# A modulation stage turned around: weight tiles as the stationary operand, condition columns streamed

## The reference

```
silu of the condition c and of the context's condition c_ctx   (two vectors of 1024)
for each of 2 layers:  m = silu(cond) @ mod_w[layer] + mod_b[layer]
    mod_w[layer]: 1024 x 6144 float32;  m is cut into six vectors of 1024:
    shift, scale and gate for the mixer, shift, scale and gate for the FFN
h = h * (1 + scale) + shift ;  x = x + gate * y
```

## Time and profile before

| | us |
|---|---|
| median of 3 runs | 5251.93 (5250.98 to 5257.39) |
| span of the profiled execution | 5251.9 |
| modulation stage in it, first matmul to next stage | 39.15 to 216.94 |
| TensorE busy over the span | 4450.2 (85%) |
| VectorE, ScalarE, GpSimd busy | 2259.8, 1628.1, 630.8 |
| matmul records of the stage (L735) | 384, 170.0 busy |
| transposes of the stage (L721) | 96, 9.5 busy |

### The profile page before, as it was taken

One profiled execution on the slowest core, in us unless ns is written; L12 is line 12 of the kernel. 1 busy time (PEld: TensorE's weight loads), 2 busy tenths in 40 slices (PEclk: granted clock), 3 DMA queues, 4 the chain that ended last, 5 costly groups with the idle time before them and its releaser, 6 DMA issues. The chain is left out here.

```text
span 5251.9 us, 53549 instructions
## 1 busy us (share of the span) xinstructions
PE 4450.2 (85%) x21497; PEld 3364.3 (64%) x21497; DVE 2259.8 (43%) x2925; ACT 1628.1 (31%) x2392; POOL 630.8 (12%) x523
## 2 busy tenths in 40 slices
PE   7797967799997887879989699976996969995997
PEld 2285545688875554657777388545785648843876
DVE  0213665311453222263362545455364455355356
ACT  0211452211342111152252233332363233233244
POOL 0000021000000011000000256100000235401000
PEclk9898977899998988989999889888998978886998
DMA  7510001111111111123222000011222100001321
GB/s 257 185 57 23 1 5 33 48 64 64 55 50 43 48 50 42 34 80 96 86 82 85 8 1 1 5 48 57 94 90 64 37 9 1 5 1 49 103 88 64
DMA packets 258876, 290.91 MB, mean 55 GB/s; under 512 B 6891, under 2 KB 230658, under 8 KB 258690
## 3 DMA queue, kind: packets, MB, share of 16 engines
q1 hardware_dynamic: 258689, 288.36, 17.0%
HBM read 286.24 MB, written 2.10 MB: 55 GB/s over the span
## 5 line engine op out<-in xcount | busy, mean ns | idle before, releaser
L421 PE MATMUL banks<-h_halves,w_halves 128*128 128x512 f32 (+1 forms) x4400 | 1627.1, 370 | 92.4 <-DVE w_halves L255 52.7
L422 PE MATMUL banks<-h_halves,w_halves 128*128 128x512 f32 (+1 forms) x4400 | 1626.4, 370 | 0.0
L423 PE MATMUL banks<-h_halves,w_halves 128*128 128x512 f32 (+1 forms) x4400 | 1617.8, 368 | 0.0
L421 PEld LDWEIGHTS banks<-h_halves,w_halves 128*128 128x128 f32 x4400 | 838.0, 190 | 255.1 <-issue 64.9
L423 PEld LDWEIGHTS banks<-h_halves,w_halves 128*128 128x128 f32 x4400 | 835.5, 190 | 141.2
L422 PEld LDWEIGHTS banks<-h_halves,w_halves 128*128 128x128 f32 x4400 | 837.7, 190 | 135.8
L255 DVE TENSOR_TENSOR w_halves<-work,w_halves 128x2048 fp32r<-128x2048 f32 (+1 forms) x215 | 492.1, 2291 | 735.9 <-ACT w_halves L250 735.9
L250 ACT ACTIVATE w_halves<-work 128x2048 fp32r<-128x2048 f32 (+1 forms) x215 | 407.4, 1896 | 292.8 <-PE banks L423 245.6
L250 ACT ACTIVATE h_halves<-kept 128x512 fp32r<-128x512 f32 (+1 forms) x520 | 336.1, 667 | 344.6 <-PE banks L423 266.9
L255 DVE TENSOR_TENSOR h_halves<-kept,h_halves 128x512 fp32r<-128x512 f32 (+1 forms) x520 | 364.9, 737 | 161.9 <-ACT h_halves L250 161.3
L526 ACT ACTIVATE kept<-banks 128x512 f32<-128x512 f32 (+1 forms) x158 | 85.7, 594 | 797.8 <-PE banks L423 797.8
(11 more groups left out here) (297 smaller groups left out, 4627.1 us busy)
## 6 DMA issues: line engine op xcount, KB each, us to landing
work<-in_w_ff SPq DMA_DIRECT2D x64, 1024.0 KB, 5.4
work<-in_mod_w SPq DMA_DIRECT2D x24, 2048.0 KB, 8.0
work<-in_ffn_w_in SPq DMA_DIRECT2D x44, 1024.0 KB, 5.1
work<-in_odd_w_in SPq DMA_DIRECT2D x24, 1024.0 KB, 5.6
work<-in_w_in SPq DMA_DIRECT2D x24, 1024.0 KB, 5.2
work<-in_ffn_w_out SPq DMA_DIRECT2D x16, 1024.0 KB, 5.1
work<-in_even_w_in SPq DMA_DIRECT2D x13, 1024.0 KB, 5.4
work<-in_odd_w_out SPq DMA_DIRECT2D x8, 1024.0 KB, 5.1
```

Source lines behind the costliest of these rows:

```text
L421: nc.tensor.matmul(o, low[:, k - a, fc], rh[:, tc], start=(k == 0), stop=False)
L422: nc.tensor.matmul(o, high[:, k - a, fc], rl[:, tc], start=False, stop=False)
L423: mm = nc.tensor.matmul(o, high[:, k - a, fc], rh[:, tc], start=False, stop=(k == K - 1))
```

## The change

The roles of the two operands are exchanged. For each tile there are 4 blocks of 128 weight columns; for each block, 8 matmuls (one for each k) whose stationary operand is the 128 x 128 block of weights and whose streamed operand is the pair of condition columns. A sum lands as 128 x 2 columns, which is the layout wanted. The 4 blocks fill 8 columns of bank j % 2 (`summed`). ScalarE's row copies, TensorE's transposes and the two semaphores for them are gone. VectorE adds the bias from the sums directly. TensorE now waits for the bias add of tile g - 2 in place of the row copy of g - 2 and the add of g - 4. The loads, the ring of three slots and the order of the tiles stay.

```diff
-    row = lambda b: core.sb(U0 + b * cols, cols, 2)
-    (in0, in1, in2, rows_summed, rows_copied, rows_turned, bias_added) = core.sems(7)
+    (in0, in1, in2, columns_summed, bias_added) = core.sems(5)
...
-    turned = lambda j: core.ps[:, 2 + j % 2, 0:8]
+    summed = lambda j: core.ps[:, j % 2, 0:8]
...
-                        sp.wait_ge(rows_summed, g - slots + 1)
+                        sp.wait_ge(columns_summed, g - slots + 1)
...
-            def turn(g, j):
-
-                for q in range(4):
-                    mm = nc.tensor.transpose(turned(j)[:, 2 * q:2 * q + 2], row(j % 2)[:, q * P:(q + 1) * P],
-                                             core.sb(IDENT0, 2, 2))
-                mm.then_inc(rows_turned, 1)
-
...
                     if later or j >= 2:
-                        pe.wait_ge(rows_copied, g - 1)
-                    if later or j >= 4:
-                        pe.wait_ge(bias_added, g - 3)
-                    for k in range(KD):
-                        mm = nc.tensor.matmul(core.ps[0:2, j % 2, 0:cols], core.sb(COND0 + 2 * k, 2),
-                                              slot(j % slots)[:, k], start=(k == 0), stop=(k == KD - 1))
-                    mm.then_inc(rows_summed, 1)
-                    if later or j >= 2:
-                        turn(g - 2, (j - 2) % body)
+                        pe.wait_ge(bias_added, g - 1)
+                    for q in range(4):
+                        for k in range(KD):
+                            mm = nc.tensor.matmul(summed(j)[:, 2 * q:2 * q + 2], slot(j % slots)[:, k, q * P:(q + 1) * P],
+                                                  core.sb(COND0 + 2 * k, 2), start=(k == 0), stop=(k == KD - 1))
+                    mm.then_inc(columns_summed, 1)
...
-        @block.scalar
-        def _(act):
-            def body_of(layer, i, later):
-                for j in range(body):
-                    g = (layer * R + i) * body + j
-                    act.wait_ge(rows_summed, g + 1)
-                    if later or j >= 2:
-                        act.wait_ge(rows_turned, g - 1)
-                    nc.scalar.activation(row(j % 2), core.ps[0:2, j % 2, 0:cols], ACT.Copy).then_inc(rows_copied, 1)
-            loop(act, body_of)
...
-                    dve.wait_ge(rows_turned, g + 1)
+                    dve.wait_ge(columns_summed, g + 1)
...
-                                            turned(j).rearrange("p (q n) -> p q n", n=2), bias,
+                                            summed(j).rearrange("p (q n) -> p q n", n=2), bias,
```

More of the change, by code:

```diff
@@ L730, in body_of @@
                     if later or j >= 2:
-                        pe.wait_ge(rows_copied, g - 1)
-                    if later or j >= 4:
-                        pe.wait_ge(bias_added, g - 3)
-                    for k in range(KD):
-                        mm = nc.tensor.matmul(core.ps[0:2, j % 2, 0:cols], core.sb(COND0 + 2 * k, 2),
-                                              slot(j % slots)[:, k], start=(k == 0), stop=(k == KD - 1))
-                    mm.then_inc(rows_summed, 1)
-                    if later or j >= 2:
-                        turn(g - 2, (j - 2) % body)
-            loop(pe, body_of)
[L741 to L744, removed]
-        @block.scalar
-        def _(act):
-            def body_of(layer, i, later):
-                for j in range(body):
-                    g = (layer * R + i) * body + j
-                    act.wait_ge(rows_summed, g + 1)
-                    if later or j >= 2:
-                        act.wait_ge(rows_turned, g - 1)
-                    nc.scalar.activation(row(j % 2), core.ps[0:2, j % 2, 0:cols], ACT.Copy).then_inc(rows_copied, 1)
-            loop(act, body_of)
+                        pe.wait_ge(bias_added, g - 1)
[4 more added lines that the diff above has]
+                    mm.then_inc(columns_summed, 1)
+            loop(pe, body_of)
         @block.vector
```

## The result

The changed kernel takes 5403.84 us (median of 4 runs, 5391.14 to 5410.21), the kernel before 5251.45 beside it (median of 4, 5250.04 to 5257.39). The ratio is 1.0287 (95% interval 1.0272 to 1.0301): slower by 2.9%, 152 us. Forecast was 5404, range 5394 to 5422.

A forecast was written before the change was run, and what follows sets the result against it. TensorE alone was taken to pace the modulation stage. To 5251.9 us came +150.8 for 1536 records at half clock and 1.2 for waits at tile heads, total +152.0: 5403.9, taken as 5404; range 5394 to 5422.

The forecast's parts named there:

- Stage on the path, each us counts: Modulation stage: the next stage starts on all engines when it ends, so each us here is one of the kernel.
- 1536 records, the load as the price: Stage's matmuls: 64 records a tile, 1536 in all, each streaming 2 columns and loading 128; only the load costs time.
- 0.2133 us at half clock: Each 128-column load in the stage: 0.2133 us at half clock, 13.65 us a tile, read from L1947.
- 0.107 to 0.115 at full clock: Each 128-column load in the stage: 0.107 to 0.115 us at full clock; 7.04 us a tile at 0.110.
- Half clock from start to end: TensorE throughout the stage: hardly anything streams, so the clock stays at half; the stage ends at 367.7, +150.8 us.
- Waits at the tile heads, 1.2 us: Head of each of 24 tiles: loads queue behind two satisfied semaphore waits, 0.05 us each tile, 1.2 us, range 0 to 4.
- Later stages within 3 us: Stages after modulation: they start 152 us later with the same state; 3 us each way allowed in the range.
- Transfers hidden: Weight transfers in the stage: 6 to 8 us each against 13.65 a tile; SP waits over 250 us for slots.
- D, an alternating clock: Rival for the stage: clock alternates between its levels, half the time at each; +71 us, 5323 us; chance 0.05.

The follow-up runs named there:

- e2: The changed kernel with 32 streamed columns in place of 2 behind each load; 5408.4 us, one run.
- e3: The changed kernel with k as the outer loop and each column block in a PSUM bank of its own; 5405.85 us, one run.
- e5: The changed kernel with 128 streamed columns per load in the first two of 24 tiles, 2 in the other 22; 5390.5 us, one run.
- e1: The changed kernel with 128 streamed columns in place of 2 behind each load; 5251.28 us, ratio 0.9995 to the kernel before the change.
- e9: The changed kernel with 64 streamed columns in place of 2 behind each load; 5403.95 us, one run.
- e6: As e4, but all 8 row matmuls of a tile come first, then its 8 column matmuls; 5302.98 us, one run.
- e4: The kernel before, with 384 columns of each tile kept as rows and 128 as a stationary block, matmuls alternating; 5303.68 us, ratio 1.0087.
- e7: As e4, but the row matmuls also use 128 stationary columns, the condition pair laid out 64 times; 5259.37 us, one run.
- e8: The kernel before, with tiles and condition split into high and low float32r parts and three products summed, low by low omitted; 5215.27 us, ratio 0.9930.

## Why the prediction was right, point by point

- **Stage on the path, each us counts.** Right: 151.0 us in the stage, 152.2 in the span.
- **1536 records, the load as the price.** Right in number; e2 and e3 show that neither stream nor sum takes part.
- **0.2133 us at half clock.** Right: 1536 x 0.2133 = 327.6, busy 327.8. Six loads of another stage (L1947, L1949) were enough, because both their spacing and their granted clock could be read.
- **0.107 to 0.115 at full clock.** Right: 0.11 in e5, 0.112 in e1. (Two times printed to 0.01 allow 0.10 to 0.12 where I wrote up to 0.115.) At full clock the change would have been hardly a gain: 7.15 us a tile in e1, which streams more, against 7.29.
- **Half clock from start to end.** Right, and for the reason given: e1 (128 columns, full), e9 (64, half), e5 (dense loads lose full clock). All of the 152 us hang on this step. The row that carried it was L1448, where the clock fell under an engine that the table shows as busy for 3.42 of 3.42 us. The Trainium skill, "TensorE: Matmul & The Clock Gate", in its closing table, asks for a TensorE kept busy continuously. In e9 both of its rows are busy for 20.00 of 20.00 us at 0.50, so by the bars of the profile that advice isn't enough. The section "LDWEIGHTS (loading the stationary operand)" of the same page of the Trainium skill puts a load at columns / 1.2 ns, an estimate of 107 ns for 128 columns. The runs agree at full clock (0.11 in e5 and e1) and not at half, where the stage has 0.213; the measurement decides.
- **Waits at the tile heads, 1.2 us.** Too much: the first load starts at 39.35 and the last at 366.77, which is 1535 x 0.2133 = 327.4 with nothing between. The last add starts 0.69 behind that, where the sum had 0.60 for a load and a matmul. Nothing is left for the heads; a wait long satisfied cost nothing that can be seen here. The 0.2 us of a later start, some 0.1 at the end and 1.2 us in later stages made up for it, so that the total is right to 0.2 us is luck. The mechanism is not: 151.0 us arose where they were forecast.
- **Later stages within 3 us.** Right as a net sum, and too narrow for single runs. The three runs before spread over 6.4 us; 15 and 11 more runs spread over 23 and 24, and the four of the changed kernel over 19. The medians agree closely, but my allowance was taken from too few runs, and one single run (5391.14) lies below my range. (My own terms add up to a range of 5395 to 5420; 5394 to 5422 is a little wider.)
- **Transfers hidden.** Right; SP waited 279.6 us, over the 250 named.
- **D, an alternating clock.** Not here. But e6 shows that it exists: tiles of 8.00 us at full clock, and others of 9.69 with a part at half.

## What to carry to other kernels

When the roles of the operands are exchanged, price the loads as well as the streams. A float32 record paid 0.11 us for 128 loaded columns and 0.43 for 512 streamed ones, so an exchange that turns 512 streamed columns into four loads of 128 comes out about even: 7.15 us a tile against 7.29, at full clock (e1). The copies and transposes that it removes are worth only what they took on the bounding engine, here 0.43 us of 7.29.

Then ask what is still streamed. With 2, 32 or 64 streamed columns behind each load of 128 the stage stayed at half clock, and started at full clock with 2 it fell back (e5), though the bars of TensorE were full. That nearly doubled the stage. Look for a stage in the same trace with short streams and read spacing and granted clock together: here L1448 and L1947 held the answer before the change was run.

## What was not expected of the hardware

- With 64 streamed columns to each 128-column float32 load the stage stayed at half clock (5403.95 us), with 128 it was at full (5251.28).
- After a stream, a load with another width of stationary operand was not hidden and came some 0.09 us late. Keeping 128 throughout took 1.4 us off a tile (e4 to e7), and 14 changes fewer took 1.26 off (e4 to e6, tiles at full clock).
- 1.9 us of loads with 2 streamed columns in each tile left the streams after them partly at half clock in some tiles and not in others (e6: 9.69 and 8.00 us a tile).
- The same pattern of streams and loads ran at half clock for 21 us and then at full (e4); what raised the clock is open.
- float32r records of 512 columns with 2 stationary columns came 0.236 us apart, with 357 GB/s of transfers as without any (e8: 5.66 and 5.65 us for 24).
